# Two-layer attention of a mixer kernel: heads in pairs, or head by head in overlapping steps

## The reference

```
q = rms_norm(q) * q_gain ; k = rms_norm(k) * k_gain        # the latent tokens are also rotated (RoPE)
s = (q @ keys.T) * 128 ** -0.5                              # keys, values: latent and context tokens
p = softmax(s)
o = p @ values
```

## Time and profile before

| what | us |
|---|---|
| median of 3 runs (2680.25 to 2683.36) | 2680.53 |
| the profiled execution, own time | 2678.77 |
| its span | 2677.0 |
| layer 0: first score product to first product of `za` | 1368.34 to 1454.75 |
| layer 0: starts of the four pairs on PE | 1368.34, 1391.82, 1413.57, 1433.65 |
| layer 1: first score product to first product of `za` | 2347.47 to 2407.79 |
| layer 1: starts of the four pairs on PE | 2347.47, 2364.66, 2378.14, 2392.91 |

### The profile page before, as it was taken

The page is one execution under the profiler, slowest core; times in us unless marked ns, Lnnn a source line. Parts: engine busy times, 40 slices in busy tenths (PEclk is TensorE's granted clock), DMA queues, the critical chain, the costliest instruction groups (busy, mean ns, idle before and its releaser), DMA issues.

```text
span 2677.0 us, 33290 instructions
## 1 busy us (share of the span) xinstructions
PE 2393.2 (89%) x13074; PEld 2068.6 (77%) x13074; DVE 1576.6 (59%) x2821; ACT 941.6 (35%) x1447; POOL 30.6 (1%) x37
## 2 busy tenths in 40 slices
PE   8899999999979778699978999998687769979996
PEld 6789988898857677688866888887476669859996
DVE  7879967799954355542353444444653555455665
ACT  5554545655421223222223322231212324334341
POOL 0000000000000000000000000000000100000000
PEclk9899989999979777799979999999897779989998
DMA  5258745377632100023300333332221005405651
GB/s 190 82 166 279 244 136 172 97 232 259 215 104 80 54 1 1 2 79 95 88 23 16 95 96 101 95 95 87 64 84 51 1 1 156 129 0 163 177 181 64
DMA packets 154708, 284.58 MB, mean 106 GB/s; under 512 B 9460, under 2 KB 34164, under 8 KB 154296
## 3 DMA queue, kind: packets, MB, share of 16 engines
q1 hardware_dynamic: 152448, 276.60, 33.3%
q10 hardware_dynamic: 2104, 5.85, 0.6%
HBM read 281.37 MB, written 1.05 MB: 105 GB/s over the span
## 4 chain that ended last, share of the span: by engine, by line
PE 75%; DVE 14%; DVEq 4%; ACT 3%; issue 2%; DMA 1%; ACTq 0%; SPq 0%
PE bank L1655 19%; PE bank L1656 19%; PE bank L1657 19%; DVE WLO L799 2%; PE bank L1960 2%; PE bank L1959 2%; PE bank L2012 1%; PE bank L2029 1%; PE bank L1860 1%; PE bank L2121 1%; PE bank L2141 1%; PE bank L2038 1%; PE bank L1932 1%; DVEq L1197 1%; DMA RAW<-in_e_w_in 1%
## 5 line engine op out<-in xcount | busy, mean ns | idle before, releaser
L799 DVE TENSOR_TENSOR WLO<-RAW,WHI 128x1024 fp32r<-128x1024 f32 (+2 forms) x500 | 583.8, 1172 | 619.6 <-ACT WHI L452 607.3
L452 ACT ACTIVATE WHI<-RAW 128x1024 fp32r<-128x1024 f32 (+2 forms) x500 | 508.6, 1018 | 1177.1 <-PE bank L1657 1137.4
L1655 PE MATMUL bank<-ATH,WHI 128*128 128x256 f32 (+1 forms) x1968 | 646.2, 328 | 37.1 <-issue 26.1
L1656 PE MATMUL bank<-ATL,WHI 128*128 128x256 f32 (+1 forms) x1968 | 642.8, 327 | 0.0
L1657 PE MATMUL bank<-ATH,WLO 128*128 128x256 f32 (+1 forms) x1968 | 642.7, 327 | 0.0
L1655 PEld LDWEIGHTS bank<-ATH,WHI 128*128 128x128 f32 x1968 | 376.6, 191 | 74.7 <-issue 33.2
L1656 PEld LDWEIGHTS bank<-ATL,WHI 128*128 128x128 f32 x1968 | 376.7, 191 | 31.0
L1657 PEld LDWEIGHTS bank<-ATH,WLO 128*128 128x128 f32 x1968 | 376.3, 191 | 31.1
L1655 PE MATMUL bank<-WHI,ATH 128*128 128x512 f32 (+2 forms) x772 | 296.8, 384 | 12.7 <-DVE WLO L799 6.0
L1656 PE MATMUL bank<-WLO,ATH 128*128 128x512 f32 (+2 forms) x772 | 293.6, 380 | 0.0
L1657 PE MATMUL bank<-WHI,ATL 128*128 128x512 f32 (+2 forms) x772 | 293.1, 380 | 0.0
(11 more groups left out here) (279 smaller groups left out, 2764.3 us busy)
## 6 DMA issues: line engine op xcount, KB each, us to landing
RAW<-in_w_in SPq DMA_DIRECT2D x192, 512.0 KB, 3.6
RAW<-in_w_ff SPq DMA_DIRECT2D x128, 512.0 KB, 4.9
ARENA<-in_w_ada SPq DMA_DIRECT2D x64, 384.0 KB, 5.0
RAW<-in_o_w_in SPq DMA_DIRECT2D x24, 512.0 KB, 3.9
RAW<-in_e_w_in SPq DMA_DIRECT2D x16, 512.0 KB, 4.8
RAW<-in_w_ple_gate SPq DMA_DIRECT2D x16, 512.0 KB, 4.2
RAW<-in_w_br_gla SPq DMA_DIRECT2D x16, 512.0 KB, 3.5
RAW<-in_w_br_attn SPq DMA_DIRECT2D x16, 512.0 KB, 3.5
```

The costliest lines, as they stand in the source:

```text
L452: nc.scalar.activation(WHI[:, slot, 0:n], RAW[:, slot, 0:n], ACT.Copy).then_inc(hi_split, 1)
L799: V.tensor_tensor(WLO[:, slot, 0:n], RAW[:, slot, 0:n], WHI[:, slot, 0:n], ALU.subtract).then_inc(lo_split, 1)
L1655: mm(o, ah, bh, start=start, stop=False, skip_group_check=free)
L1656: mm(o, ah, bl, start=False, stop=False, skip_group_check=free)
```

## The change

- The heads go one by one. On ACT and DVE `exps_of`, `turned_out` and `maxima` hold the same instructions as `attend` did, for one head; on PE `scores` does. In step n the score products are those of head n, the turn and value products those of head n - 1, and DVE stores head n - 2. Each engine has one list of such steps in place of the four pairs. The score banks are still 0 to 2 and 3 to 5, by the parity of the head.
- The value products write bank 6, and the rotation products bank 7 alone.
- DVE no longer multiplies the probabilities. It multiplies the identity matrix by the reciprocals, one 128x128 diagonal matrix for each query tile (`DIAGP`, in the room of the keys' first buffer). PE's transposes become matrix products of the block with that diagonal matrix, which turn and divide at once.
- Ahead of the loop only head 0 gets `gain` and `rotate`, not heads 0 and 1.

```diff
+        DIAGP = at(10240 + AH * TOK, 2 * TT * P, "p (r t n) -> p r t n", r=2, t=TT)
@@ ACT
-                for _ in range(AH // 2):
-                    attend()
+                def exps_of(r):
...
+                def turned_out(r):
...
+                for n in range(AH + 1):
+                    if n:
+                        turned_out((n - 1) % 2)
+                    if n < AH:
+                        exps_of(n % 2)
@@ DVE
-                for r in range(2):
-                    gain(r, r)
+                gain(0)
...
-                for r in range(2):
-                    rotate(r)
+                rotate(0)
+                def maxima(hd):
...
+                def divide(r):
+                    dve.wait_ge(a_exp, T.next(a_exp))
+                    V.reciprocal(RD[:, r, 0:nq], DN[:, r, 0:nq])
+                    drain()
+                    for t in range(nq):
+                        last = V.tensor_scalar(DIAGP[:, r, t, :], ident, RD[:, r, t:t + 1], None, ALU.mult)
+                    last.then_inc(a_norm, 1)
+                def stored(hd):
+                    dve.wait_ge(a_out, T.next(a_out))
+                    V.tensor_copy(QG[:, bass.ds(hd * TOK, tq)], bank[6][:, 0:tq]).then_inc(a_stored, 1)
+                for n in range(AH + 2):
+                    if 1 <= n <= AH:
+                        divide((n - 1) % 2)
+                    if n < AH:
+                        maxima(n)
+                    if n >= 2:
+                        stored(n - 2)
+                    if n + 1 < AH:
+                        gain(n + 1)
+                        rotate((n + 1) % 2)
@@ PE
+                def turn_probs(r):
+                    pe.wait_ge(a_norm, T.next(a_norm))
+                    for t in range(NT):
+                        for s in range(TT):
-                                last = turn(bank[3 * r + t][:, s * P:(s + 1) * P], PL[:, r, t, s * P:(s + 1) * P], ident)
+                            last = mm(bank[3 * r + t][:, s * P:(s + 1) * P], PL[:, r, t, s * P:(s + 1) * P], DIAGP[:, r, t, :], start=True, stop=True)
...
+                    last.then_inc(a_turned, 1)
+                def values(hd, kv):
+                    r, v = hd % 2, [VA[:, s, kv * AD:(kv + 1) * AD] for s in range(TT)]
+                    pe.wait_ge(a_pt, T.next(a_pt))
+                    if hd:
+                        pe.wait_ge(a_stored, T.next(a_stored))
...
+                for n in range(AH + 1):
+                    if n < AH:
+                        scores(n % 2, n * AKV // AH)
+                    if n:
+                        turn_probs((n - 1) % 2)
+                    if n + 1 < AH:
+                        rotated(bank[7][:, 0:S], QS[:, (n + 1) % 2, 0:S])
+                    if n:
+                        values(n - 1, (n - 1) * AKV // AH)
+                pe.wait_ge(a_stored, T.next(a_stored))
```

More of the change, by code:

```diff
@@ L742, in _ @@
                 segment(f"v{layer}", [4])
-                def attend():
-                    for r in range(2):
[L747 to L753, removed]
-                    for r in range(2):
[L755 to L762, removed]
@@ L764, in _ @@
-                for _ in range(AH // 2):
-                    attend()
+                def exps_of(r):
+                    act.wait_ge(a_max, T.next(a_max))
+                    for t in range(nq):
+                        dst, src = (PL[:, r, t, :], bank[3 * r + t][:, :]) if t < NT else \
+                            (PC[:, r, t - NT, :], bank[3 * r + 2][:, (t - NT) * S:(t - NT + 1) * S])
+                        last = nc.scalar.activation(dst, src, ACT.Exp, bias=NM[:, r, t:t + 1], scale=SCL[:, r, t:t + 1],
+                                                    accum_out=DN[:, r, t:t + 1])
+                    last.then_inc(a_exp, 1)
@@ new lines, in turned_out @@
+                def turned_out(r):
+                    act.wait_ge(a_turned, T.next(a_turned))
+                    for t in range(NT):
+                        last = nc.scalar.activation(PLT[:, r, :, t * P:(t + 1) * P],
+                                                    bank[3 * r + t][:, :].rearrange("p (s n) -> p s n", s=TT), ACT.Copy)
+                    if nq > NT:
+                        last = nc.scalar.activation(PCT[:, r, :, :].rearrange("p s (t n) -> p s t n", t=NT),
+                                                    bank[3 * r + 2][:, :].rearrange("p (t s n) -> p s t n", t=NT, s=NT), ACT.Copy)
+                    last.then_inc(a_pt, 1)
@@ L1512, in _, with gain @@
                 drain()
-                def gain(r, hd):
-                    V.tensor_scalar(QS[:, r, 0:tq], QG[:, bass.ds(hd * TOK, tq)], col("q_norm_g_2", layer), None, ALU.mult).then_inc(a_gain, 1)
+                def gain(hd):
+                    V.tensor_scalar(QS[:, hd % 2, 0:tq], QG[:, bass.ds(hd * TOK, tq)], col("q_norm_g_2", layer), None, ALU.mult).then_inc(a_gain, 1)
                 def rotate(r):
                     dve.wait_ge(a_rot, T.next(a_rot))
-                    V.tensor_tensor(ROTW[:, r, :], cst("sin"), bank[6 + r][:, 0:S], ALU.mult)
+                    V.tensor_tensor(ROTW[:, r, :], cst("sin"), bank[7][:, 0:S], ALU.mult)
                     V.tensor_tensor(QS[:, r, 0:S], QS[:, r, 0:S], cst("cos"), ALU.mult)
@@ L1582, in _ @@
-                for i in range(AH // 2 - 1):
-                    attend(i * 2, True)
-                attend(AH - 2, False)
+                rotate(0)
+                def maxima(hd):
+                    r = hd % 2
+                    dve.wait_ge(a_score, T.next(a_score))
+                    for t in range(nq):
+                        sc = bank[3 * r + t][:, :] if t < NT else bank[3 * r + 2][:, (t - NT) * S:(t - NT + 1) * S]
+                        V.tensor_reduce(NM[:, r, t:t + 1], sc, AX, ALU.max, negate=True)
+                    V.tensor_copy(SCL[:, r, 0:nq], RSQ[:, bass.ds(hd * nq, nq)])
+                    drain()
+                    V.tensor_tensor(NM[:, r, 0:nq], NM[:, r, 0:nq], SCL[:, r, 0:nq], ALU.mult).then_inc(a_max, 1)
@@ L2105, in _ @@
                 rotated(bank[5][:, :], KG[:, :, 0:S])
-                for r in range(2):
-                    rotated(bank[6 + r][:, 0:S], QS[:, r, 0:S])
+                rotated(bank[7][:, 0:S], QS[:, 0, 0:S])
                 pe.wait_ge(a_diag, T.next(a_diag))
@@ L2112, in _ @@
                 last.then_inc(a_bc, 1)
[L2114 to L2131, removed]
-                                last = turn(bank[3 * r + t][:, s * P:(s + 1) * P], PL[:, r, t, s * P:(s + 1) * P], ident)
[L2133 to L2139, removed]
-                        for s in range(TT):
[L2141 to L2146, removed]
-                        pe.wait_ge(a_stored, T.next(a_stored))
@@ L2149, in _, with scores @@
[L2149 to L2153, removed]
+                def scores(r, kv):
+                    pe.wait_ge(a_q, T.next(a_q))
+                    for t in range(nq):
+                        q = QS[:, r, t * P:(t + 1) * P]
+                        if t < NT:
+                            last = mm(bank[3 * r + t][:, :], q, K2[:, kv, :], start=True, stop=True)
+                        else:
+                            last = mm(bank[3 * r + 2][:, (t - NT) * S:(t - NT + 1) * S], q, K2[:, kv, S:TOK], start=True, stop=True)
+                    last.then_inc(a_score, 1)
@@ new lines, in turn_probs @@
+                def turn_probs(r):
+                    pe.wait_ge(a_norm, T.next(a_norm))
+                    for t in range(NT):
+                        for s in range(TT):
+                            last = mm(bank[3 * r + t][:, s * P:(s + 1) * P], PL[:, r, t, s * P:(s + 1) * P], DIAGP[:, r, t, :], start=True, stop=True)
+                    for t in range(nq - NT):
+                        for s in range(NT):
+                            last = mm(bank[3 * r + 2][:, t * S + s * P:t * S + (s + 1) * P], PC[:, r, t, s * P:(s + 1) * P], DIAGP[:, r, NT + t, :], start=True, stop=True)
+                    last.then_inc(a_turned, 1)
@@ new lines, in values @@
+                def values(hd, kv):
+                    r, v = hd % 2, [VA[:, s, kv * AD:(kv + 1) * AD] for s in range(TT)]
+                    pe.wait_ge(a_pt, T.next(a_pt))
+                    if hd:
+                        pe.wait_ge(a_stored, T.next(a_stored))
+                    for s in range(TT):
+                        last = mm(bank[6][:, 0:S], v[s], PLT[:, r, s, :], start=s == 0, stop=s == TT - 1)
+                    if nq > NT:
+                        for s in range(NT):
+                            last = mm(bank[6][:, S:TOK], v[NT + s], PCT[:, r, s, :], start=s == 0, stop=s == NT - 1)
+                    last.then_inc(a_out, 1)
```

## The result

| | before | changed |
|---|---|---|
| median of 10 runs, us | 2680.72 (2679.2 to 2684.12) | 2686.36 (2685.17 to 2694.54) |
| ratio to before | | 1.0023 (95% interval 1.0014 to 1.0033) |
| span of the profiled execution | 2677.0 | 2683.3 |
| layer 0, first score product to first product of `za` | 86.4 | 1367.47 to 1458.39 = 90.9 |
| layer 1, the same | 60.3 | 2351.08 to 2414.22 = 63.1 |

The change makes the kernel 0.23% slower. The two attentions explain it: +4.5 and +2.8 us, less 0.9 us by which layer 0's attention starts earlier, are 6.5 us; the span of the profiled execution is 6.3 longer, the median of the runs 5.6.

A forecast was written before the change was run, and what follows sets the result against it. PE was taken to bound the kernel, busy 68.6 of layer 0's 86.4 us, partly at its low clock. Layer 0's +3.7 and layer 1's +2.7 us gave +6.4, so 2686.9 us; range 2680 to 2695.

The forecast's parts named there:

- The turn: PE's diagonal products, two instructions a block at 0.11 us: 2.6 us a head for 1.3 in layer 0.
- The factor of four: Rival for PE's diagonal products: four times the transposes' cost, 5.3 us a head, +41 us, 2722; chance 0.02.
- The step: In the loop, from one head's scores to the next's: 9.8 us in layer 0, 6.7 in layer 1.
- PE's waits mainly for ACT's copies, none for maxima: Expected sign in the trace after: inside the attentions PE waits mainly for copies of turned blocks; no size given.
- The filling: Pipeline start: layer 0's head 1 scores start at 9.9 us, at the low clock, ending at 15.0; layer 1 11.2.
- the 0.8 us for a first turn at the low clock: Layer 1, after the filling: a turn at the low clock adds 0.8 us to the attention.
- The clock inside the steps: In the loops PE keeps the full clock, as it never pauses for over 0.9 us.
- the rival in which it rises sooner: While filling, the clock rises sooner: +1.0 us in total, 2681.5, or +3.3, 2683.8, if midway; chance 0.22.
- the one in which it falls in the loop: Clock falls in the loop or draining: one fall in each layer at the end gives +10.4, 2690.9; chance 0.17.
- Ahead of layer 0's loop: Before layer 0's scores, one gain leaves DVE's chain to the norms, saving 0.44 us.
- a turn of one instruction: Rival: the diagonal product is one instruction like the transpose; layers 83.7 and 59.3 us, -4.4, 2676.1; chance 0.08.
- the doubled turn takes the overlap back: In the loop, the doubled turn and unhidden copies take most of the overlap's gain: 9.8 us against 10.05 to 11.75.

The follow-up runs named there:

- the overlap alone: The changed kernel with PE's transposes and DVE's division of the probability tiles put back: 2684.29 us, ratio 1.0013 to before.
- the best version: Overlapping steps with transposes and DVE's division, each next head's gain ahead of the maxima, head 1 prepared ahead of the loop: 2662.47 us, ratio 0.9927 to before.
- gain early: The overlap alone with the gain of head n + 1 moved ahead of the maxima of head n on DVE: 2668.14 us, ratio 0.9945 to before.
- head 1 ahead: The changed kernel with head 1's gain, rotation product and rotate done ahead of the loop: 2680.21 us, ratio 0.9997 to before.

## Why the prediction was right

The time was 2686.4 us against 2686.9, and the mechanism was the forecast one. The terms of layer 0 hold one by one; those of layer 1 hold in sum.

- The turn: 24 instructions a head, PE at its work from 1402.74 to 1405.4. The price of 0.11 us each and the count of two were right. The factor of four that the Trainium skill gives ("TensorE: Matmul & The Clock Gate", section Terms) was not: with transposes the turn takes 1.3 us, half of it.
- The step: 9.78 and 6.67 us against 9.8 and 6.7. The order of its ends was right: value products last released by ACT, rotation products in the gap at 1406.25 (3.5 us after the scores, as worked out), division early. The sign "PE's waits mainly for ACT's copies, none for maxima" did not come out: in a step PE waits 0.67 us for the gain, which DVE does behind maxima and store, and 0.29 for the copies. The sum had this wait inside the gap ahead of the value products, which the copies end, so the step's length does not depend on it.
- The filling: head 1's scores started 10.3 us after head 0's, against 9.9, and the clock had fallen, as forecast; layer 0 came to 90.9 against 90.5. Layer 1 was 63.1 against 63.3, but here two terms missed and cancelled: until the end of head 1's scores it took 11.9 us against 11.2, and the 0.8 us for a first turn at the low clock were not spent (16 products in 1.95 us from 2362.96). That much is luck.
- The clock inside the steps stood, as forecast from the kernel before. So the rival in which it rises sooner is out, but for layer 1's first turn, and so is the one in which it falls in the loop.
- Ahead of layer 0's loop 0.9 us went in place of 0.44, of which 0.40 is the removed gain: from the rotation products at 1354.85 (before) and 1354.38 to the first scores it is 13.49 and 13.09 us. The other 0.47 lie ahead of the changed code. The 0.3 us forecast for layer 1 did not show: from the end of layer 0's attention to the start of layer 1's it is 892.7 us in both kernels.

Where the prediction was wrong is in a rival. It priced a turn of one instruction at 10.8 us less, with the clock held (83.7 and 59.3 us). The runs with transposes in this loop show 1 to 2 us: the diagonal products' second instruction had covered 1.3 us of PE's pause, and without it the pause grew from 0.67 to 2.04 us and the low clock took back 7 us in layer 0. With the clock held by useless work the same loop takes 84.9 and 60.5 us, 8.7 less than the changed one. So the sentence that the doubled turn takes the overlap back is right only for a loop in which the clock holds without it: it costs 9 us in this one and 16 in the best. The shown causes of the lost gain are then: the fold (16.2 us in the best loop), the gain behind the maxima (16 us with the clock it costs, in the overlap alone, and nothing with the fold), and the filling (5.7 to 6.2 us, by the best version against gain early, and by head 1 ahead against the changed kernel). These prices do not add up: from the changed kernel to the best version it is 24 us, as the early gain pays only once the fold is gone, and the fold's removal pays in full only with the early gain.

## What to carry to other kernels

Before folding a vector operation into a TensorE operation, compare the two forms of the TensorE operation in the trace, instruction counts first: fp32 products came as two instructions and transposes as one. In a software pipeline, put on each engine's list first what another engine needs soonest and the engine itself has long been able to do; here one moved line on DVE was worth 16 us with transposes, and nothing while the doubled turn covered it. Price a shorter operation together with the pause that it leaves behind: if TensorE pauses longer for it, the clock may take the gain back.

## What the hardware showed that I had not expected

- Less PE work made the kernel no faster, and useless PE work made it 5 to 7 us faster. In this loop pauses of 2.04 to 2.36 us behind a turn of 1.3 us brought the clock down in four of five steps of layer 0; pauses of 1.41 to 1.77 us in its layer 1, of 1.30 to 1.74 in the best version's layer 0, or of 0.74 behind useless work, in none.
- Between products, transposes hold the clock up as well as more products do: 84.9 us of layer 0 with either. The Trainium skill says otherwise on its page "TensorE: Matmul & The Clock Gate" (Part 4: PE-mode transpose): that the full clock does not engage for transposes, since they don't count as work in the same way. The measurement disagrees for fp32 transposes of 128x128: 12 of them in 1.47 us, added to a step's pause, kept it at 1.00 where it fell without them.
